# Moving a ScalarE copy from the start of one pass to the end of the pass before, and spreading TensorE's filler matmuls anew, in a gated-delta-net core

## The chip, the cores and the metric

The kernel runs on 1 core of one Trainium2 chip. The metric is the device time in microseconds (us) of one execution, taken as the median of several.

## The reference, cut to what matters

An encoder of two layers works on two sequences of 256 tokens with 1024 features, in float32. Layer 0 mixes tokens with multi-head attention, layer 1 with a gated delta net (GDN) that runs in both directions. Each layer then has a mixture of 16 experts with expert-choice routing, and a gated projection. The change lies inside the GDN of layer 1, whose core is this:

```python
L = jnp.where(strict, jnp.einsum('bhncd,bhnsd->bhncs', kb, k) * decay, 0.0)
T = lax.linalg.triangular_solve(eye + L, eye, left_side=True, lower=True)
u = T @ vb
w = T @ (kb * jnp.exp(gc)[..., None])
...
def step(state, inp):                       # over the chunks of a sequence
    v_new = u_n - w_n @ state
    o_n = qg_n @ state + a_n @ v_new
    state = state * gl_n[..., None, None] + jnp.swapaxes(kg_n, -1, -2) @ v_new
```

The output of the core is gated with `silu(z)`, where `z` is one slice of the input projection `h @ w_in`. This projection of `z` is independent of the core.

## The kernel before

The kernel keeps activations on chip and streams all weights from memory. Each engine has its own instruction list, written out by hand, and semaphores join the lists. An engine works its list strictly in order, so a wait at one instruction holds all that stand behind it.

**The core in passes.** The work of the core is cut into `QS = 4` passes. A pass `q` covers 16 units: 4 heads, two directions, two sequences, of 128 tokens. For every pass the triangular matrix is inverted by doubling. Level 0 is done on VectorE; levels 1 to 4 work inside 32x32 blocks; two more steps (`z5`, `du5`, `dt5` and `z6`, `du6`) join the blocks to 64 and to 128. Then `vn`, `av`, `ks`, `qs` and `st` apply the inverse. The loop `for p in range(QS + 1)` runs levels 0 to 4 of pass `p` and, between them, the joins and the application of pass `p - 1` (`prev`). TensorE, ScalarE and VectorE each have such a loop, in `gdn_pe`, `gdn_act` and `gdn_dve`. A boundary between iterations is called p=0 to p=1, and so on.

**One level.** TensorE transposes the unfinished inverse (`level_turn`, L1414) and multiplies it with the matrix (`level_z`, L1405). ScalarE spreads the transposed inverse into a block-diagonal buffer (`spread_u`, L932, four copies), and VectorE transposes the product (`turn_z`, L2103). TensorE multiplies both (`level_d`, L1427). VectorE puts the result in place and transposes it (`merge`: L2112 and L2087; the latter counts the semaphore `t1_done`), and the next `level_turn` may start.

**Between two passes.** After `level_d(p, 4)` TensorE has `build_qk(p, 2)` and `build_qk(p, 3)` (L1377), `level_turn(p+1, 0)`, `level_z(p+1, 1)`, then `z5(p)` (L1445), which waits for the last `merge` of pass `p`, `level_d(p+1, 1)`, `du5(p)` (L1456), which waits until ScalarE has copied the result of `z5` (`keep`, L964), `dt5(p)` (L1466), the next level, and `z6(p)` (L1480, L1481), which waits for `join64` (L960, L961). On ScalarE `end_levels(q)` (L944) copies the finished 32x32 blocks of pass `q` into the buffer `c_t64`, four copies of 32x256; `join64` adds the off-diagonal blocks to it. `end_levels` waits for `t1_done` of the last level and, from pass 1 on, for `z6` of the pass before, which is the last reader of `c_t64`. `spread_inverse` (L953) copies the same blocks into `c_u`.

**The filler of p=0.** In p=0 there is no earlier pass, and TensorE fills the gaps of the levels with the projection of `z`: eight groups `gate_part(i, k0, k1)` (L1346), of eight matmuls each, from `xt` and a weight slot. Each of these matmuls stands as two records in the trace. ScalarE takes each finished group out with `gate_in(i)` (L885). Groups 5, 6 and 7 are the ones within p=0.

**GpSimd.** The buffer `xt` is used again once the projection is done. The list of GpSimd (POOL) has this at that point:

```python
pool.wait_ge(*s_z.full(8))                       # all eight groups of z are done
pool.memset(flat_xt, 0.0).then_inc(zeroed, 1)    # L699
pool.wait_ge(zeroed, 3)
spread_m(1)                                      # L674, four copies into xt
mask_decay(1)
```

For p=1 and later, `level_z(p, 1)` waits for `spread_m(p)`, and `spread_u(1, 0)` on ScalarE waits for the memset (`zeroed` at 3), since both kinds of block-diagonal buffer lie in `xt` from pass 1 on.

Of the kernel before, what the change touches and what calls it, by code (L numbers as in the profile page):

```python
# [21 lines left out]
KD = D // P  # L22
# [101 lines left out]
def trunk_kernel(nc, x_prompt, x_sample, p_prompt, p_sample, norm_mix_g, norm_ffn_g, norm_ple_g,  # L124
# [4 lines left out]
    with ExitStack() as ctx:  # L129
# [266 lines left out]
        for l in range(2):  # L396
# [3 lines left out]
            prev = lay[0] if l else None  # L400
# [369 lines left out]
        def _(act):  # L770
# [68 lines left out]
            def gdn_act():  # L839
# [41 lines left out]
                def gate_in(i):  # L881

                    f, j = i // 4, i % 4
                    act.wait_ge(*s_z.full(i + 1))
                    act.activation(znat[:, j, 4 * f:4 * f + 4, :], psum[:, apply_banks.bank(s_z, i), :].rearrange("p (h w) -> p h w", h=4),  # L885
                                   ACT.Silu).then_inc(s_z.freed(i)[0], 1)
# [48 lines left out]
                def end_levels(q):  # L935

                    act.wait_ge(t1_done, t1_at(q, LEVELS - 1))
                    if q:
                        act.wait_ge(*core["z6"].full(q))
                    if q == 0:  # L940
                        act.wait_ge(zeroed, 2)
                    for g in range(4):
                        gs, u0 = slice(32 * g, 32 * g + 32), 8 * (g // 2)
                        ins = act.activation(c_t64[gs, :, 32 * (g % 2):32 * (g % 2) + 32], c_t1[q % 2][gs, u0:u0 + 8, :], ACT.Copy)  # L944
                    ins.then_inc(t64_done, 1)
# [52 lines left out]
                for p in range(QS + 1):  # L998
                    live, prev = p < QS, p - 1
                    m_prev = prev % 2  # L1000
                    if live:
                        spread_u(p, 0)
                    if p:
                        end_levels(prev)
                        keep(apply_banks, "z5", prev, c_z5, 32)
                        spread_inverse(prev)
                    else:
                        gate_in(5)
                    if p:
                        join64(prev)  # L1010
                        if p == QS:
                            act.wait_ge(o_sum, 1)
                            act.activation(fac[:, F_Y, :, 0:4], fac[:, F_Y, :, 0:4], ACT.Sqrt).then_inc(o_sqrt, 1)
                    if live:
                        spread_u(p, 1)
                    if p:
                        keep(apply_banks, "z6", prev, c_z6, 64)
                    else:
                        exp_decay(1, 0)
                        exp_decay(1, 1)  # L1020
                    if p >= 2 and p % 2 == 0:
                        for a in range(4):
                            keep(apply_banks, "st", 4 * (p // 2 - 1) + a, c_s[a // 2][:, 4 * (a % 2):4 * (a % 2) + 4, :], P)
                    if p in (1, 2):
                        exp_decay(p + 1, 0)
                    if live:
                        spread_u(p, 2)
                    if p == 0:
                        exp_decay(1, 2)
                        exp_decay(1, 3)  # L1030
                    if p == QS - 1:
                        square_out(0, 0)
                        square_out(0, 1)
                    if p and m_prev == 0:
                        for a in (0, 1):
                            keep(apply_banks, "vn", 4 * prev + a, c_vn[:, 4 * a:4 * a + 4, :], P)
                    if p in (1, 2):
                        exp_decay(p + 1, 1)
                        exp_decay(p + 1, 2)
                    if p and m_prev == 0:  # L1040
                        for a in (2, 3):
                            keep(apply_banks, "vn", 4 * prev + a, c_vn[:, 4 * a:4 * a + 4, :], P)
                    if p == QS - 1:
                        square_out(0, 2)
                        square_out(0, 3)
                    if p and m_prev == 1:
                        for a in range(4):
                            keep(apply_banks, "vn", 4 * prev + a, c_vn[:, 4 * a:4 * a + 4, :], P)
                    if p in (1, 2):
                        exp_decay(p + 1, 3)  # L1050
                    if live:
                        spread_u(p, 3)
                    if p + 1 < QS:
                        start_level(p + 1)
                    if p == 0:
                        gate_in(6)
                        gate_in(7)

                def turned(k):

# [97 lines left out]
        def _(pe):  # L1158
# [143 lines left out]
            def gdn_pe():  # L1302
# [237 lines left out]
                for p in range(QS + 1):  # L1540
                    live, prev = p < QS, p - 1
                    odd = prev % 2
                    build = p in (1, 2)
                    if live:
                        level_turn(p, 0)
                        level_z(p, 1)
                    if p:
                        z5(prev)
                    else:
                        gate_part(5, 0, 5)  # L1550
                    if live:
                        level_d(p, 1)
                    if p:
                        du5(prev)
                        dt5(prev)
                    else:
                        gate_part(5, 5, KD)
                        gate_part(6, 0, 1)
                    if live:
                        level_turn(p, 1)  # L1560
                        level_z(p, 2)
                    if p:
                        z6(prev)
                    else:
                        gate_part(6, 1, 4)
                        build_kk(1, 0)
                    if p >= 2:
                        for a in range(4):
                            if p % 2 == 0:
                                new_state(p - 2, a)  # L1570
                            else:
                                with_state("qs", p - 2, a)
                            if p == QS and a == 1:
                                du6(prev)
                    if live:
                        level_d(p, 2)
                    if 1 <= p < QS:
                        du6(prev)
                    elif p == 0:
                        gate_part(6, 4, 7)  # L1580
                        build_kk(1, 1)
                    if build:
                        build_kk(p + 1, 0)
                    if live:
                        level_turn(p, 2)
                        level_z(p, 3)
                    if p and odd:
                        for a in range(4):
                            with_state("ks", prev, a)
                    elif p:  # L1590
                        for a in (0, 1):
                            new_values(prev, a)
                    else:
                        gate_part(6, 7, KD)
                        gate_part(7, 0, 2)
                        build_kk(1, 2)
                    if build:
                        build_kk(p + 1, 1)
                        build_kk(p + 1, 2)
                    if live:  # L1600
                        level_d(p, 3)
                    if p == QS:
                        for a in range(4):
                            with_state("qs", prev, a)
                    if p:
                        for a in range(4) if odd else (2, 3):
                            new_values(prev, a)
                    else:
                        gate_part(7, 2, 5)
                        build_kk(1, 3)  # L1610
                    if build:
                        build_kk(p + 1, 3)
                    if live:
                        level_turn(p, 3)
                        level_z(p, 4)
                    if p == QS:
                        turn_heads(0)
                    if p:
                        for a in range(4):
                            attend(prev, a)  # L1620
                    else:
                        gate_part(7, 5, KD)
                    if live:
                        build_qk(p, 0)
                        build_qk(p, 1)
                        level_d(p, 4)
                        build_qk(p, 2)
                        build_qk(p, 3)
                def project_heads(i, half):
# [791 lines left out]
```

## Time and profile before

| what | value |
|---|---|
| median of 3 runs | 1781.27 us (1781.05 to 1781.36) |
| profiled execution, its own time | 1781.27 us |
| span of the profiled execution | 1779.5 us |
| TensorE (PE) busy | 1638.2 us, 92% |
| VectorE (DVE), ScalarE (ACT), GpSimd (POOL) busy | 515.8, 461.7, 67.5 us |
| iteration p=0 of the core | from 973.5 to 1016.7 us of the span |
| passes p=1 to p=4 | up to about 1166 us |

PE is the matrix engine, and PEld is the loading of its weights, which overlaps with it. A row of a timeline gives the start in the span, the busy time, engine, line of the kernel, operation and operands, then the number of instructions merged into the row, and in brackets how long the engine stood idle before it and what ended that.

### The profile page before, as it was taken

The page shows a single profiled execution, that of the slowest core. Times are in us where ns is not written, and L with a number is a line of the kernel's source. Part 1 is how long each engine was busy: PE and PEld are TensorE (multiplying, and loading weights), DVE is VectorE, ACT ScalarE, POOL GpSimd, SP SyncE. Part 2 cuts the span into 40 slices and gives each one's busy share as a digit, 9 for nine tenths or more (in the row PEclk, how much of TensorE's full clock was granted, in tenths as well). Part 3 has the DMA queues.
Part 4 walks back from the last instruction along what each step waited for, and adds up shares of the span by engine and source line. Part 5 has one row for each costly group of instructions (what it writes and reads, how often), then busy time and mean ns, then how long its engine had stood idle before and what let it go on. Part 6 is the DMA issues. An engine that isn't in the chain of part 4 may idle for free.

```text
span 1779.5 us, 20467 instructions
## 1 busy us (share of the span) xinstructions
PE 1638.2 (92%) x8671; PEld 774.6 (44%) x8671; DVE 515.8 (29%) x998; ACT 461.7 (26%) x1008; POOL 67.5 (4%) x87
## 2 busy tenths in 40 slices
PE   7999799998899979999999999897999988999887
PEld 4464344342243324444445678753443422433233
DVE  3562401120111213254451356633111202112032
ACT  3232211110011105432225575442111010111053
POOL 2000000000000000000004231000000000000000
PEclk9999899999999999999999999998999999999999
DMA  7007269999999995012120000273699999999931
GB/s 249 1 6 325 119 282 427 428 428 428 427 424 429 427 424 188 0 48 93 49 95 1 1 3 2 96 300 150 245 427 428 427 428 427 424 429 426 427 138 47
DMA packets 50906, 450.30 MB, mean 253 GB/s; under 512 B 4931, under 2 KB 7199, under 8 KB 25599
## 3 DMA queue, kind: packets, MB, share of 16 engines
q1 hardware_dynamic: 50288, 448.67, 60.9%
q8 instruction: 69, 1.13, 0.3%
q0 software_dynamic: 288, 0.22, 0.0%
q14 instruction: 22, 0.18, 0.0%
q10 hardware_dynamic: 239, 0.09, 0.0%
HBM read 446.87 MB, written 2.10 MB: 252 GB/s over the span
## 4 chain that ended last, share of the span: by engine, by line
PE 74%; DMA 16%; ACT 5%; DVE 3%; issue 1%; SPq 1%; DVEq 0%; ACTq 0%
PE banks L1726 26%; PE banks L1184 23%; DMA ring<-in_moe_w_up 7%; DMA ring<-in_moe_w_down 5%; PE banks L1377 4%; DMA ring<-in_moe_w_gate 3%; PE banks L1635 3%; PE banks L1346 3%; PE banks L1752 3%; PE banks L1705 3%; PE banks L1780 2%; PE banks L1267 1%; PE banks L1386 1%; PE banks L1405 1%; PE banks L1427 1%
## 5 line engine op out<-in xcount | busy, mean ns | idle before, releaser
L1726 PE MATMUL banks<-ring,misc 128*64 128x512 f32 x2048 | 460.1, 600 | 38.6 <-DMA ring<-in_moe_w_up 21.7
L1726 PEld LDWEIGHTS banks<-ring,misc 128*64 128x64 f32 x2048 | 147.1, 138 | 324.3 <-issue 280.9
L1726 PE MATMUL banks<-ring,hid_t 128*64 128x512 f32 x976 | 218.1, 596 | 17.8 <-DMA ring<-in_moe_w_down 15.1
L1184 PE MATMUL banks<-ring,xt 128*128 128x512 f32 (+1 forms) x448 | 189.8, 586 | 1.1 <-ACT xt L763 0.6
L2357 DVE TENSOR_TENSOR work<-work,banks 128x512 f32<-128x512 f32 x32 | 33.7, 1053 | 483.6 <-PE banks L1726 483.6
L1184 PE MATMUL banks<-xt,ring 128*128 128x512 f32 x384 | 166.7, 594 | 0.0
L1134 ACT ACTIVATE misc<-banks 32x512 f32<-32x512 f32 x64 | 37.5, 586 | 463.7 <-PE banks L1726 463.3
L1726 PEld LDWEIGHTS banks<-ring,hid_t 128*64 128x64 f32 x976 | 68.5, 137 | 158.1 <-issue 136.6
L1184 PEld LDWEIGHTS banks<-ring,xt 128*128 128x128 f32 x448 | 84.9, 190 | 103.9 <-issue 102.9
L1184 PEld LDWEIGHTS banks<-xt,ring 128*128 128x128 f32 x384 | 72.4, 190 | 91.8 <-issue 89.3
L2372 DVE COPY misc<-banks 32x512 f32<-32x512 f32 x64 | 44.2, 691 | 228.6 <-PE banks L1726 228.2
L1121 ACT ACTIVATE work<-banks 128x512 f32<-128x512 f32 x32 | 19.1, 597 | 221.8 <-PE banks L1726 221.8
L2023 DVE SCALAR_TENSOR_TENSOR misc<-misc,conv_w 128x512 f32<-128x512 f32 x96 | 72.2, 752 | 3.4
L1752 PE MATMUL banks<-misc,xt 128*128 128x512 f32 x128 | 62.2, 620 | 5.4 <-ACT misc L1134 3.1
L1705 PEld LDWEIGHTS banks<-xt,xn 128*128 128x128 f32 x512 | 61.5, 202 | 11.3 <-DVE xt L2318 6.4
L1705 PE MATMUL banks<-xt,xn 128*128 128x128 f32 x512 | 62.9, 287 | 3.3 <-DVEq L2321 3.3
L1346 PE MATMUL banks<-ring,xt 128*128 128x512 f32 x128 | 57.5, 598 | 0.0
L1377 PEld LDWEIGHTS banks<-ring 128*128 128x128 f32 x384 | 48.2, 197 | 14.1 <-issue 9.3
L1377 PE MATMUL banks<-ring 128*128 128x128 f32 x384 | 51.2, 284 | 3.1 <-DVE ring L2078 1.4
L2347 DVE TENSOR_TENSOR h<-h,banks 128x512 f32<-128x512 f32 x64 | 43.6, 687 | 14.1 <-PE banks L1752 14.1
L737 ACT ACTIVATE work<-h 128x512 f32<-128x512 f32 x40 | 24.8, 620 | 76.9 <-DVE h L1977 42.6
L1104 ACT ACTIVATE misc<-banks,ffn_gains 128x256 f32<-128x256 f32 x32 | 13.4, 470 | 109.8 <-PE banks L1705 109.8
(311 smaller groups left out, 1515.2 us busy)
## 6 DMA issues: line engine op xcount, KB each, us to landing
ring<-in_moe_w_gate SPq DMA_DIRECT2D x64, 2048.0 KB, 22.2
ring<-in_moe_w_up SPq DMA_DIRECT2D x64, 2048.0 KB, 24.0
ring<-in_moe_w_down SPq DMA_DIRECT2D x58, 2048.0 KB, 25.5
ring<-in_gdn_w_in SPq DMA_DIRECT2D x8, 2048.0 KB, 8.5
ring<-in_ple_w_gate SPq DMA_DIRECT2D x4, 2048.0 KB, 21.4
ring<-in_moe_w_down SPq DMA_DIRECT2D x6, 1024.0 KB, 23.2
ring<-in_mla_w_out SPq DMA_DIRECT2D x2, 2048.0 KB, 23.6
misc<-in_moe_w_down SPq DMA_DIRECT2D x2, 2048.0 KB, 21.3
```

The source lines that it names most:

```text
L1134: ins = act.activation(ybuf[32 * i:32 * i + 32, s, 0:HALF], psum[32 * s:32 * s + 32, 5, :], ACT.Copy)
L1184: mm = pe.matmul(psum[:, banks.bank(st, i), 0:cols], lhs(k), rhs(k), start=(k == 0), stop=(k == n - 1))
L1346: mm = pe.matmul(psum[:, apply_banks.bank(s_z, i), :], xt[:, k, j * P:(j + 1) * P], slot(6 + f, KD, HALF)[:, k, :], start=(k == 0), stop=( ...
L1377: mm = pe.matmul(o, lhs(g), rhs(g), start=True, stop=True)
L1635: mm = pe.matmul(psum[:, banks.bank(s_go, i), :], got[:, k, j * P:(j + 1) * P], gw_out[f][:, k, :], start=(k == 0), stop=(k == KD - 1))
L1705: mm = pe.matmul(o, xn[:, NT * s + t, c0:c0 + P], oh[:, NT * s + t, q * P:(q + 1) * P], start=(t == 0), stop=(t == NT - 1))
L1726: mm = pe.matmul(psum[64 * f:64 * f + 64, bank, :], tokens(4 * kh + k), w[k][:, k, f * HALF:(f + 1) * HALF], start=(kh == 0 and k == 0), s ...
L1752: pe.matmul(psum[:, 6 + g % 2, :], sc[:, q, j, :], ybuf[:, j // NT, f * HALF:(f + 1) * HALF], start=True, stop=True).then_inc(moe_sem["sca ...
L1780: mm = pe.matmul(psum[:, b, :], ptt(l)[:, k, j * P:(j + 1) * P], w_proj(l)[:, k, f * HALF:(f + 1) * HALF], start=(k == 0), stop=(k == 1))
L2023: ins = dve.scalar_tensor_tensor(out=a, in0=x, scalar=w, in1=a, op0=ALU.mult, op1=ALU.add)
L2347: dve.tensor_tensor(hv, hv, psum[:, 6 + g % 2, :], ALU.add).then_inc(moe_sem["scat_free"], 1)
L2372: ins = dve.tensor_copy(ybuf[32 * i:32 * i + 32, s, HALF:D], psum[64 + 32 * s:96 + 32 * s, 5, :])
```

## The change

Two things are moved; no instruction is added or removed.

On ScalarE, `end_levels` of a pass no longer stands in the next iteration, behind `spread_u(p+1, 0)`, but as the last thing of its own iteration, behind `start_level(p+1)` and, in p=0, behind `gate_in(6)` and `gate_in(7)`.

On TensorE, the 24 filler matmuls of p=0 are cut in another way. Before, the gaps took 5, 4, 3, 3, 3, 3 and 3 of them, all ahead of `level_d(0, 4)`. Now they take 5, 3, 2, 2, 2, 2 and 4, and the last 4 stand behind `level_d(0, 4)`, ahead of `build_qk(0, 2)`.

```diff
 def gdn_act():
     for p in range(QS + 1):
                     if live:
                         spread_u(p, 0)
                     if p:
-                        end_levels(prev)
                         keep(apply_banks, "z5", prev, c_z5, 32)
                         spread_inverse(prev)
...
                     if p == 0:
                         gate_in(6)
                         gate_in(7)
+                    if live:
+                        end_levels(p)
 def gdn_pe():
                         gate_part(5, 5, KD)
-                        gate_part(6, 0, 1)
...
-                        gate_part(6, 1, 4)
+                        gate_part(6, 0, 2)
                         build_kk(1, 0)
...
-                        gate_part(6, 4, 7)
+                        gate_part(6, 2, 4)
                         build_kk(1, 1)
...
-                        gate_part(6, 7, KD)
-                        gate_part(7, 0, 2)
+                        gate_part(6, 4, 6)
                         build_kk(1, 2)
...
-                        gate_part(7, 2, 5)
+                        gate_part(6, 6, KD)
                         build_kk(1, 3)
...
-                        gate_part(7, 5, KD)
+                        gate_part(7, 0, 4)
                     if live:
                         build_qk(p, 0)
                         build_qk(p, 1)
                         level_d(p, 4)
+                        if p == 0:
+                            gate_part(7, 4, KD)
                         build_qk(p, 2)
                         build_qk(p, 3)
```

## Rows read from the trace of the kernel before

**Rows 1.** The page: busy time of the engines, and DMA in 40 slices.

```profile
PE 1638.2 (92%) x8671; PEld 774.6 (44%) x8671; DVE 515.8 (29%) x998; ACT 461.7 (26%) x1008; POOL 67.5 (4%) x87
...
DMA  7007269999999995012120000273699999999931
```

**Rows 2.** Waits from 1008 to 1165 us: waiter, releaser, total, times, longest.

```profile
PE banks L1456 <- ACT misc L964: 4.3, 4, 1.2
...
PE banks L1427 <- ACT xt L932: 2.3, 3, 1.3
...
PE banks L1405 <- POOL xt L674: 0.7, 1, 0.7
```

**Rows 3.** Timeline of PE, in p=0 and at the boundary to p=1.

```profile
980.88 3.70 PE L1346 MATMUL banks<-ring,xt 128*128 128x512 f32 x8
...
1008.96 2.84 PE L1346 MATMUL banks<-ring,xt 128*128 128x512 f32 x6
...
1013.51 1.08 PE L1427 MATMUL banks<-xn,misc 128*32 128x128 f32 x32
...
1018.09 1.08 PE L1405 MATMUL banks<-xt,misc 128*32 128x128 f32 x32 [0.70 <-POOL xt L674]
1019.10 1.11 PE L1445 MATMUL banks<-misc,ring 32*32 32x32 f32 x64
...
1022.21 1.01 PE L1456 MATMUL banks<-misc 32*32 32x32 f32 x58 [0.99 <-ACT misc L964]
...
1028.06 1.08 PE L1427 MATMUL banks<-xt,misc 128*32 128x128 f32 x32 [1.26 <-ACT xt L932]
```

**Rows 4.** Timeline of ACT at the same boundary.

```profile
1017.43 2.39 ACT L932 ACTIVATE xt<-banks 32x512 f32<-32x512 f32 x4 [1.50 <-PE banks L1414]
1019.84 1.69 ACT L944 ACTIVATE misc<-misc 32x256 f32<-32x256 f32 x4
1021.56 0.60 ACT L964 ACTIVATE misc<-banks 128x512 f32<-128x512 f32 x1
1022.18 2.54 ACT L953 ACTIVATE ring<-misc 32x512 f32<-32x512 f32 x4
...
1025.53 2.39 ACT L932 ACTIVATE xt<-banks 32x512 f32<-32x512 f32 x4
```

**Rows 5.** Timeline of POOL at the same boundary.

```profile
1011.86 3.51 POOL L699 MEMSET xt<- 128x4096 f32 x1 [35.61 <-PE banks L1346]
1015.44 2.60 POOL L674 COPY xt<-ring 32x512 f32<-32x512 f32 x4
```

**Rows 6.** Timeline of DVE, ACT and PE at p=1 to p=2.

```profile
1054.92 0.71 DVE L2087 STREAM_TRANSPOSE misc<-misc 128x512 f32<-128x512 f32 x1
...
1055.29 2.39 ACT L932 ACTIVATE xt<-banks 32x512 f32<-32x512 f32 x4 [5.50 <-PE banks L1414]
...
1057.70 1.69 ACT L944 ACTIVATE misc<-misc 32x256 f32<-32x256 f32 x4
1057.82 1.08 PE L1427 MATMUL banks<-xt,misc 128*32 128x128 f32 x32 [0.52 <-ACT xt L932]
...
1060.07 1.01 PE L1456 MATMUL banks<-misc 32*32 32x32 f32 x58 [1.16 <-ACT misc L964]
```

**Rows 7.** Timeline of ACT at p=3 to p=4.

```profile
1134.24 1.69 ACT L944 ACTIVATE misc<-misc 32x256 f32<-32x256 f32 x4 [4.19 <-DVE misc L2087]
```

**Rows 8.** Timeline of PE: a slow `level_z`, and two long gaps elsewhere.

```profile
748.53 1.09 PE L1166 MATMUL banks<-ident,xn 128*128 128x128 f32 x8 [2.48 <-ACT xn L746]
...
1107.13 1.93 PE L1405 MATMUL banks<-xt,misc 128*32 128x128 f32 x32
...
1559.27 3.53 PE L1726 MATMUL banks<-ring,misc 128*64 128x512 f32 x8 [4.81 <-DMA ring<-in_moe_w_up]
```

**Rows 9.** Windows: busy of PE, PEld, DVE, ACT, POOL, then PE's granted clock, DMA.

```profile
1559.50:1562.90 3.40, 3.40 (x10) 0.98 (x8) 0.00 (x0) 0.00 (x0) 0.00 (x0) 0.50 1.01 429
1105.50:1108.90 3.40, 3.40 (x51) 2.62 (x47) 1.68 (x4) 3.31 (x7) 0.00 (x0) 0.50 0.02 5
```

## The prediction

> **What bounds the kernel now.** I read the page first, then the waits of the core, then the timelines of the engines around each place that the diff touches, and last the granted clock. On the page the reader is to see that PE is busy for 1638.2 us of 1779.5, and that DMA is idle while the core runs and at its full share after it [rows 1]. The expert stage behind the core starts from the core's end, since its weights go into buffers that the core frees, so I take it that a microsecond gained or lost on PE's path through the core moves the end by one. The waits of the core show where PE stands still at pass boundaries: 4.3 us in four waits of `du5` for ACT's copy of `z5`, 2.3 us in three waits of `level_d` for `spread_u`, and once 0.7 us of `level_z` for POOL [rows 2]. ACT works in order, so what stands ahead of the awaited copy on its list matters. At p=0 to p=1 that is `end_levels`: `z5` starts at 1019.10 and lasts 1.11, so its result is there at 1020.21, but ACT is in `end_levels` until 1021.53, copies at 1021.56, and `du5` starts only at 1022.21 [rows 3, 4]. That is what the edit on ACT aims at. But the same boundary has a second chain, of POOL: the last group of z ends at 1008.96 + 2.84 = 1011.80, the memset of `xt` starts at 1011.86, the copies into it run from 1015.44 to 1018.04, and `level_z(1, 1)` starts at 1018.09, 0.05 behind them [rows 3, 5]. This chain has no slack at all: whatever delays the last group of z delays `level_z(1, 1)`.
>
> **The change at p=0 to p=1.** Number and size of the matmuls stay. One filler matmul is 3.70 - 2.84 = 0.86 us, a run of four against a run of three [rows 3]. Within p=0, PE has work in every gap, and with one filler less in most gaps the levels simply follow each other sooner; the ACT part of a level is 2.39 us [rows 4] and the gap still holds two fillers and a `build_kk`, so I cost that at nothing. If this cover were too thin, each of the five thinned gaps could add some tenths. `level_d(0, 4)` then comes four fillers earlier, at 1013.51 - 3.44 = 1010.1. Level products take PE 1.01 until the next starts (1018.09 to 1019.10 [rows 3]), so the last four fillers begin at 1011.1 and end 3.70 later, at 1014.8, where the last group of z ended at 1011.80. So z is complete 3.0 us later. Behind this event stand POOL's memset, its copies, `mask_decay(1)`, and on ACT `gate_in(7)`, then the moved `end_levels(0)`, then `spread_u(1, 0)`.
>
> POOL: memset 1014.9 to 1018.4 (3.51), copies to 1021.0 (2.60) [rows 5], `level_z(1, 1)` at 1021.1 in place of 1018.09, 3.0 later. PE has only `build_qk` and `level_turn(1, 0)` to do from 1014.8; before, `level_z` could have started at 1018.09 - 0.70 = 1017.4, 2.9 behind the time at which `level_d(0, 4)` let the next one go (1013.51 + 1.01) [rows 3], so PE is done with them by 1017.5 at the latest and stands idle for nearly 4 us. ACT: `end_levels(0)` ends at about 1017.2 and is hidden in this wait; `spread_u(1, 0)` waits for the memset, 1018.4, and ends at 1020.8 (2.39), ahead of need. Then `z5` starts 1.01 behind `level_z`, at 1022.1, and ends at 1023.2. ACT is free and copies at once, at 1023.2 in place of 1021.56: 1.7 later. So the `end_levels` that is gone from this chain pays back 1.3 of the 3.0 (1021.53 less 1020.21), and no more. From there ACT's list is the path as before: `spread_inverse` and `join64` up to `spread_u(1, 1)` at 1025.53, whose end releases `level_d(1, 2)` at 1028.06 behind 1.26 us of idle time [rows 3, 4]. With 1.7 more, `level_d(1, 2)` starts at 1029.8. This boundary: **+1.7 us**.
>
> **The change at the later boundaries.** At p=1 to p=2 no filler is moved, but the place of `end_levels` is. It waits for the last transposition of `merge(1, 4)`, which DVE ends at 1054.92 + 0.71 = 1055.63; `spread_u(2, 0)`, free to go at 1055.29 before, now stands behind it [rows 6]. New: `end_levels(1)` 1055.65 to 1057.34 (1.69), `spread_u(2, 0)` to 1059.75 (2.39), `level_d(2, 1)` at 1059.9 in place of 1057.82, 2.07 later, with PE idle for 2.6 us ahead of it. `du5` is next on PE, 1.01 behind, at 1060.9; the copy of `z5`, at 1059.8 to 1060.4, is ready by then, so the wait of 1.16 us for it is gone. Against 1060.07 that is **+0.83 us**. So the edit turns a wait of 1.16 into one that is 2.07 longer, since 1.69 us of copies are put ahead of an operation that PE needs 2.5 us sooner than `z5`'s copy. The wait of `du5` occurs four times with at most 1.2 us each [rows 2], and p=2 to p=3 has the same order and distances as p=1 to p=2, so I count it with **+0.83 us** again. At p=3 to p=4 there is no `spread_u(4, 0)`; `end_levels(3)` stands behind `spread_u(3, 3)` in both versions and waits for DVE [rows 7]: **0**. The copies themselves are as many as before. Sum of the waits: 1.7 + 0.83 + 0.83 = 3.4 us.
>
> **The clock.** The half level, 1.2 GHz, has a price that the trace shows: from 1105.50 to 1108.90 the granted clock is 0.50 [rows 9], and a `level_z` there takes 1.93 us against 1.08 at 2.4 GHz [rows 3, 8]. The new idle time of 4 us at the first boundary has a near relative: after 4.81 us without work, PE's clock is at 0.50 from 1559.50 on [rows 8, 9]; after 2.48 us at 746, the next eight transpositions took a normal 1.09 [rows 8]. I expect the half clock in part of `level_z(1, 1)`, `z5`, `level_d(1, 1)`. Bounds: nothing, or two slowed level products, 2 x 0.85 = 1.7; I take one, 0.85. The new 2.6 us at p=1 to p=2 lies near the gap without a fall, but the clock did fall in the trace at p=2 to p=3 with shorter gaps; bounds again 0 and 1.7, I take 0.7. At p=2 to p=3 the fall is there already, so nothing new. The Trainium skill ("TensorE: Matmul & The Clock Gate", section "HAM oscillation — how this bites in real kernels") says that a long enough pause of the matrix engine brings it back to the half clock, so that the work behind a wait starts slow. By that rule the first boundary pays; without it the sum would be 1784.7. The trace agrees at the gap of 4.81 us, and doesn't settle 2.6 us.
>
> **The sum.** 3.4 + 0.85 + 0.7 = 4.95 us. The profiled execution's own time, 1781.27 us, equals the median (1781.27), so the forecast is 1781.27 + 4.95 = **1786.2 us**, +0.28%. What a measurement of this kernel can tell from no change is about 0.2%, that is 3.6 us: the forecast is outside, but not by much.
>
> **The rivals.**
> - *Waits alone, no new half clock*: +3.4, 1784.7 us. For it: the clock stayed at full through the boundaries of p=0 to p=1 and p=1 to p=2 before, in spite of 0.7, 0.99 and 1.26 us of idle time in a row. Against it: 4 us is much longer. Chance 0.2; it lies on the border of 0.2%.
> - *One boundary less*: when everything behind comes later, the half-clock stretch at 1105.50 may fall elsewhere or not happen (its price there was up to 1.3: one level product 0.85 and transpositions), or the 0.83 at p=2 to p=3 is covered by it. Then 3.4 - 1.3 = +2.1, 1783.4 us. Chance 0.12.
> - *Faster, the edit does what it aims at*: `end_levels` is done while ACT would idle anyway, and the waits of `du5` go. Price: 1.3 at the first boundary and 1.16 at two others, 3.6 us, 1777.7 us. It decides at the last `merge`: `end_levels` would have to be finished when `level_turn(p+1, 0)` releases `spread_u`, at 1055.29, so the transposition would have to end at 1053.6 and not at 1055.63; and at the first boundary POOL's copies would have to end by 1018.0, with z complete 3.0 us later. ACT's 5.50 us of idle time ahead of `spread_u(2, 0)` [rows 6] speaks for it at first sight, but it lies before the event that `end_levels` needs. Chance 0.05.
> - *Worse*: both boundaries pay the full 1.7 for the clock, 1781.27 + 3.4 + 3.4 = 1788.1 or more. Chance 0.05.
>
> **How the numbers follow.** The forecast's own case, waits plus some half clock, has 0.58, and its bounds are 1785.2 to 1787.8. The range goes from the third case (1783.4) to nearly the worst (1788.0), which leaves out under 2 in 10. Faster by over 0.2%: 0.04 (the faster rival, nearly whole). Slower by over 0.2%, above 1784.8: the forecast's case, the worst case, and nearly half of the border case, 0.58 + 0.05 + 0.08 = 0.71. Within 0.2%: 0.25.
>
> **What the changed profile would show.** Last filler of z ending at about 1014.8; memset of POOL at about 1014.9 and its copies ending at about 1021.0; `level_z(1, 1)` at 1021.1, behind some 4 us of idle time released by POOL; the wait of `du5` for the copy of `z5` gone at the first three boundaries and kept at the last; `spread_u(2, 0)` behind `end_levels`, and PE idle for 2.6 us ahead of `level_d(2, 1)` for it; a granted clock of 0.50 within about 1018 to 1025. I am wrong if `level_z(1, 1)` starts by 1019.5, if `level_d(2, 1)` is not later against `level_z(2, 1)` than before, or if a thinned gap of p=0 shows idle time on PE.

## The result and the profile after

The changed kernel takes 1790.73 us (median of 5 runs, 1790.04 to 1790.94) against 1781.10 for the kernel before, 9.6 us more: ratio 1.0054, 95% interval 1.0040 to 1.0067. The forecast was 1786.2 with a range up to 1788.0. The direction was right, the size was not. The profiled execution took 1791.96 us, and that of the kernel before 1781.27.

The page of the changed kernel. PE's busy time rose by 6.7 us although it does the same work [rows 1]:

```profile
span 1790.2 us, 20467 instructions
PE 1644.9 (92%) x8671; PEld 781.4 (44%) x8671; DVE 515.9 (29%) x998; ACT 461.8 (26%) x1008; POOL 67.5 (4%) x87
...
PEclk9999899999999999999999999998999999999999
```

Timeline of PE at p=0 to p=1. The lines of the kernel behind the edit have moved by one: L1406 is `level_z`, L1446 `z5`, L1428 `level_d`, L1457 `du5`.

```profile
1011.56 3.70 PE L1347 MATMUL banks<-ring,xt 128*128 128x512 f32 x8
...
1016.88 0.60 PE L1415 MATMUL banks<-ident,misc 128*128 128x128 f32 x4
1021.54 1.93 PE L1406 MATMUL banks<-xt,misc 128*32 128x128 f32 x32 [4.07 <-POOL xt L674]
1023.41 1.74 PE L1446 MATMUL banks<-misc,ring 32*32 32x32 f32 x64
1025.08 1.94 PE L1428 MATMUL banks<-xt,misc 128*32 128x128 f32 x32
1026.94 1.58 PE L1457 MATMUL banks<-misc 32*32 32x32 f32 x58
...
1030.99 1.94 PE L1406 MATMUL banks<-xt,misc 128*32 128x128 f32 x32
...
1034.65 1.08 PE L1428 MATMUL banks<-xt,misc 128*32 128x128 f32 x32
```

POOL and ACT there:

```profile
1015.32 3.51 POOL L699 MEMSET xt<- 128x4096 f32 x1 [38.62 <-PE banks L1347]
1018.89 2.60 POOL L674 COPY xt<-ring 32x512 f32<-32x512 f32 x4
```

```profile
1015.91 1.70 ACT L944 ACTIVATE misc<-misc 32x256 f32<-32x256 f32 x4
1018.92 2.38 ACT L932 ACTIVATE xt<-banks 32x512 f32<-32x512 f32 x4 [1.31 <-POOL xt L699]
1025.19 0.60 ACT L964 ACTIVATE misc<-banks 128x512 f32<-128x512 f32 x1 [3.88 <-PE banks L1446]
1025.82 2.55 ACT L953 ACTIVATE ring<-misc 32x512 f32<-32x512 f32 x4
1030.05 0.37 ACT L960 ACTIVATE misc<-banks 32x256 f32<-32x256 f32 x1 [1.69 <-PE banks L1467]
...
1031.09 2.39 ACT L932 ACTIVATE xt<-banks 32x512 f32<-32x512 f32 x4 [0.28 <-PE banks L1415]
```

The core starts 0.46 us later in this execution than in the one before (its first `level_turn` at 974.30 against 973.84), which has to be taken off every comparison. Then the chain is the forecast one, to a tenth: z complete at 1015.26, 3.0 late after that correction; POOL's memset and copies behind it, as long as before [rows 5]; `level_z(1, 1)` 3.45 - 0.46 = 2.99 late behind 4.07 us of idle time. What follows is not. `level_z` takes 1.93 in place of 1.08, `z5` 1.74 in place of 1.11 [rows 3], and so on up to `z6`. The windows (columns: length, PE busy, PE's granted clock, DMA share and GB/s) show it; the clock stands at 1.2 GHz, half, for 13.6 us:

```profile
1020.80:1034.40 13.60, 12.86 (x288) 0.50 0.01 4
...
1113.10:1119.80 6.70, 6.70 (x119) 0.50 0.01 2
1147.20:1153.90 6.70, 5.85 (x85) 0.50 0.52 160
```

The kernel before has half clock for 3.4 us at the boundary of the second of these rows [rows 9], and at that of the third:

```profile
1139.60:1143.00 3.40, 3.04 (x37) 0.50 0.09 29
```

Both kernels have 3.4 us more of it late in the core, behind a wait of 2.00 us for DVE (from 1156.7 on before, from 1167.5 on in the changed kernel).

At p=1 to p=2, ACT and then PE. `end_levels(1)` waits for DVE, `spread_u` stands behind it, and PE idles for 2.62 us ahead of `level_d(2, 1)`; the next boundary repeats it with 2.61:

```profile
1062.27 1.69 ACT L944 ACTIVATE misc<-misc 32x256 f32<-32x256 f32 x4 [5.88 <-DVE misc L2088]
1063.98 2.39 ACT L932 ACTIVATE xt<-banks 32x512 f32<-32x512 f32 x4
1066.39 0.60 ACT L964 ACTIVATE misc<-banks 128x512 f32<-128x512 f32 x1
```

```profile
1066.51 1.08 PE L1428 MATMUL banks<-xt,misc 128*32 128x128 f32 x32 [2.62 <-ACT xt L932]
1067.52 1.01 PE L1457 MATMUL banks<-misc 32*32 32x32 f32 x58
...
1111.25 1.08 PE L1428 MATMUL banks<-xt,misc 128*32 128x128 f32 x32 [2.61 <-ACT xt L932]
1114.82 1.11 PE L1415 MATMUL banks<-ident,misc 128*128 128x128 f32 x4
1115.86 1.94 PE L1406 MATMUL banks<-xt,misc 128*32 128x128 f32 x32
```

Where the time went, from the starts of the same instructions in both traces, each difference less the one before it (`turn_heads`, L1528 before, is PE's first work on the finished output of the core):

| stretch, up to the start of | measured | forecast, waits + clock |
|---|---|---|
| `level_d(1, 2)` (1034.65 - 1028.06 - 0.46) | +6.13 | 1.7 + 0.85 |
| `level_d(2, 2)` (1075.82 - 1068.43 = 7.39) | +0.80 | 0.83 + 0.7 |
| `level_d(3, 2)` (1123.47 - 1113.83 = 9.64) | +2.25 | 0.83 + 0 |
| first `turn_heads` behind the core (1172.53 - 1162.13 = 10.40) | +0.76 | 0 |

That is 9.94 us over the core.

### The profile page after: what moved, and what is told of

Same layout as the page of the kernel before. It is cut to its first block, busy times and chain, and to the rows that moved or that the text cites. A ratio compares the mean times of both kernels' runs of the same rounds, so it can differ in the third digit from the quotient of the medians.

```text
span 1790.2 us, 20467 instructions
## 1 busy us (share of the span) xinstructions
PE 1644.9 (92%) x8671; PEld 781.4 (44%) x8671; DVE 515.9 (29%) x998; ACT 461.8 (26%) x1008; POOL 67.5 (4%) x87
## 4 chain that ended last, share of the span: by engine, by line
PE 72%; DMA 16%; ACT 4%; DVE 3%; issue 3%; POOL 1%; SPq 1%; DVEq 0%; ACTq 0%; POOLq 0%
PE banks L1727 26%; PE banks L1185 23%; DMA ring<-in_moe_w_up 7%; DMA ring<-in_moe_w_down 5%; PE banks L1378 4%; DMA ring<-in_moe_w_gate 3%; PE banks L1636 3%; PE banks L1706 3%; PE banks L1753 3%; PE banks L1781 2%; PE banks L1347 2%; PE banks L1268 1%; PE banks L1406 1%; PE banks L1428 1%; ACT xn L737 1%
```

## The experiments

All times are medians, with the kernel before run on the same chip (1780.8 to 1781.3 us in these groups; there are three chips, and the ratio is taken within one). Where no interval is given, a difference of two medians is known to about 2 us: the intervals of the ratios are 3 to 5 us wide, and the core alone starts anywhere from 972.1 to 974.6 us in the profiled executions, though no edit lies ahead of it. The starts inside the traces, each counted from the first `level_turn` of its own core, say more, and are given where they settle something. "Mean clock" is PE's granted clock averaged from 970 to 1175 us of the span, the whole core; 0.01 less means 4.1 us more at half clock. `ident` and `tri` are constants, and the unused matmuls write into PSUM banks that the next product overwrites.

| kernel | time, us | ratio to before (95% interval) | mean clock |
|---|---|---|---|
| before | 1781.1 | | 0.98 |
| changed | 1790.7 | 1.0054 (1.0040 to 1.0067) | 0.93 |
| fillers only | 1787.0 | 1.0035 (1.0022 to 1.0049) | 0.94 |
| `end_levels` only | 1788.5 | 1.0041 (1.0028 to 1.0055) | 0.95 |
| changed, PE kept busy in the first gap | 1789.1 | 1.0041 (1.0027 to 1.0054) | 0.93 |
| changed, shorter first wait | 1788.3 | 1.0043 (1.0027 to 1.0058) | 0.94 |
| changed, PE kept busy in all gaps | 1781.4 | 1.0003 (0.9994 to 1.0012) | 1.00 |
| before, PE kept busy | 1777.8 | 0.9983 (0.9974 to 0.9992) | 0.99 |
| `end_levels` only, PE kept busy | 1780.4 | 0.9995 (0.9986 to 1.0004) | 1.00 |
| fillers only, PE kept busy | 1780.3 | 0.9986 (0.9977 to 0.9995) | 0.99 |
| before, copies on VectorE | 1776.7 | 0.9979 (0.9970 to 0.9988) | 0.97 |
| before, copies on POOL | 1774.1 | 0.9965 (0.9951 to 0.9978) | 0.98 |
| the same, PE kept busy | 1775.0 | 0.9965 (0.9951 to 0.9978) | 0.99 |

**Each half alone.** First the changed kernel with `end_levels` back in its old place:

```diff
-                    if live:
-                        end_levels(p)
...
+                        end_levels(prev)
                         keep(apply_banks, "z5", prev, c_z5, 32)
```

> The filler matmuls as in the changed kernel, end_levels at its old place in ScalarE's list. Theory (most of the loss is the half clock that follows PE's wait of 4 us for GpSimd at the first boundary): level_z(1, 1) again starts 3.0 us late, end_levels(0) is done before z5's result is there, so the first boundary loses the same 6.1 us as the changed kernel; the boundaries p=1 to p=2 and p=2 to p=3 lose nothing. Total +6 to +7 us, 1787 to 1788. Rival (the loss is mostly the new place of end_levels, whose copies delay ScalarE at each boundary): at most +2 us, below 1783.5.

Measured: 1787.0, in the expected range, but by luck of the sum. In its trace `level_z(1, 1)` is 3.0 late as expected; the loss is spread differently: 3.8 us up to `level_d(1, 2)` in place of 6.1, 2.9 more at p=1 to p=2, where nothing was changed and the clock now falls, and 1.4 less at p=2 to p=3, where the half clock of the kernel before is absent. The wait ahead of `level_z(1, 1)` is as long as in the changed kernel, and the half clock with it is half as long:

```profile
1021.14 1.93 PE L1405 MATMUL banks<-xt,misc 128*32 128x128 f32 x32 [4.07 <-POOL xt L674]
```

```profile
1019.90:1026.70 6.80, 5.56 (x134) 0.50 0.01 2
```

Then the kernel before with the ACT edit alone:

```diff
-                        end_levels(prev)
                         keep(apply_banks, "z5", prev, c_z5, 32)
...
+                    if live:
+                        end_levels(p)
```

> end_levels at its new place, the fillers as before. Theory: POOL's chain is as before; at p=0 to p=1 end_levels(0) waits for the last merge (1017.8) and puts spread_u(1, 0) 2 us later, and du5 0.9 us later; the same 0.83 at the next two boundaries: +2.5 us of waits, with no gap on PE over 2.7 us, so little new half clock except where it was before (p=2 to p=3, p=3 to p=4, 0 to 2 us more). Total +2.5 to +4.5 us, 1783.6 to 1785.6. Rival (each move costs in proportion, the clock has no part): 0.83 per boundary and nothing else, +2.5 us exactly. Rival 2 (end_levels was the main loss): +6 us or more.

Measured: 1788.5 (1785.6 to 1790.2), a miss: three times the 2.5 us of waits. Its profiled execution was the fastest of its five, 1785.6. The two halves cost 6.2 and 7.7 us by the medians and 5.9 each by the starts in the traces up to `turn_heads`, together 11.8 and more, where both edits cost 9.9. Of this excess 0.86 was to be expected, since the wait that the ACT edit adds at the first boundary is covered by POOL's when both are made. The rest points to something shared, and both traces show the clock falling at boundaries.

**PE kept busy in the first gap.**

```diff
                     level_banks.claim(pe, st, i)
                     b = level_banks.bank(st, i)
+                    if i == 4:                      # level_z(1, 1)
+                        for _ in range(4):
+                            pe.matmul(psum[:, b, :], ident[:, :], tri[:, :, :], start=True, stop=True)
                     if v == 1:
                         pe.wait_ge(m32_done, 4 * q + 4)
```

> The changed kernel, and ahead of level_z(1, 1), where PE waits about 4 us for GpSimd, four extra matmuls of 128x512 into the bank that level_z overwrites; they compute nothing that is used. They take 3.4 us and fit in the wait. Theory (half clock after the wait): PE's clock stays at full through the first boundary, level_d(1, 2) comes 1.7 to 2.2 us late instead of 6.1, and the total falls by 4 to 4.5 us against the changed kernel, to about 1786.5. Rival (the waits themselves are longer than I worked out, or PE's small matmuls are slow for another cause): added work on PE gains nothing, 1790.7 or more.

Measured: 1789.1. The total missed, the first boundary did not. Timeline of PE (here L1404 the unused matmuls, L1409 `level_z`, L1431 `level_d`):

```profile
1016.08 3.60 PE L1404 MATMUL banks<-tri,ident 128*128 128x512 f32 x8
1020.31 1.08 PE L1409 MATMUL banks<-xt,misc 128*32 128x128 f32 x32 [0.64 <-POOL xt L674]
...
1028.99 1.08 PE L1431 MATMUL banks<-xt,misc 128*32 128x128 f32 x32 [0.40 <-ACT xt L932]
...
1060.85 1.93 PE L1431 MATMUL banks<-xt,misc 128*32 128x128 f32 x32 [2.61 <-ACT xt L932]
```

The clock stays at full, and `level_d(1, 2)` starts at 1028.99 where it started at 1028.06 before; this core began 0.77 us earlier, so it is 1.70 late: the forecast 1.7. But the clock then falls at the next boundary, behind the 2.61 us, where it had not fallen in the changed kernel: the stretch to `level_d(2, 2)` loses 4.9 us in place of 0.8, and up to `turn_heads` it is 9.7 us late, where the changed kernel was 9.9. In this execution the filled gap saved next to nothing in sum while the next one was open. It is one of the slower ones (1790.2); two of the five took 1786.6 and 1786.7, the time expected, at a higher mean clock of the whole execution (0.982 and 0.983 against 0.980). They left no trace, so whether the next fall was missing in them isn't shown.

**A shorter wait.** The clearing of `xt` is shared out, and ACT's `spread_u` waits for VectorE's half (`ux_zeroed`):

```diff
-                pool.memset(flat_xt, 0.0).then_inc(zeroed, 1)
+                pool.memset(flat_xt[:, 0:2048], 0.0).then_inc(zeroed, 1)
...
                         merge(p, 4)                 # VectorE
+                        if p == 0:
+                            dve.wait_ge(*s_z.full(8))
+                            dve.memset(flat_xt[:, 2048:4096], 0.0).then_inc(ux_zeroed, 1)
```

> The changed kernel, but POOL clears only the half of xt that its own copies need (1.75 us in place of 3.51), and VectorE, idle then, clears the half that spread_u needs. Theory (the half clock follows the length of PE's wait): the wait ahead of level_z(1, 1) shrinks from 4.1 to 2.3 us, level_z(1, 1) comes 1.2 us late against the kernel before; ScalarE's chain is ahead, so the copy of z5 loses nothing. The clock falls for less than 13.7 us or not at all; total 3 to 7 us below the changed kernel, 1784 to 1788. Rival (the half clock comes at such a boundary with any gap over 2 us, and its length doesn't depend on the gap): only 1.8 us below the changed kernel, 1789.

Measured: 1788.3, 2.5 below the changed kernel; the least that I expected was 3, and the rival said 1.8, so the total doesn't decide between them. The trace says more: with 2.36 us of wait the half clock at the first boundary lasted 3.4 us in place of 13.6, and `level_d(1, 2)` is 1.11 late after the start's shift of 0.72. But 3.7 us went at the next boundary, with the clock down again.

**PE kept busy in all gaps, and the control.** The same four matmuls, and a helper that puts others into the bank of the next product:

```diff
+                def idle_work(name, i, n):
+                    if n:
+                        apply_banks.claim(pe, core[name], i)
+                    for _ in range(n):
+                        pe.matmul(psum[:, apply_banks.bank(core[name], i), :], ident[:, :], tri[:, :, :], start=True, stop=True)
...
                         z5(prev)
+                        idle_work("du5", prev, [0, 0, 2, 2, 0][p])
...
+                        idle_work("du5", prev, [0, 0, 0, 0, 1][p])
                         du5(prev)
...
+                        idle_work("z6", prev, [0, 0, 0, 0, 1][p])
                         z6(prev)
...
+                    if p == 1:
+                        idle_work("du6", prev, 1)
                     if live:
                         level_d(p, 2)
```

> The changed kernel with unused matmuls in every gap over 0.9 us up to p=4: four ahead of level_z(1, 1), one ahead of level_d(1, 2), two ahead of level_d(2, 1) and level_d(3, 1), one ahead of du5(3) and z6(3), each into a bank that the next product overwrites. With one gap filled the half clock moved on to the next boundary and the total stayed. Theory (idle time sets the clock, and the clock is what lies beyond the 3.4 us of waits): full clock through the core up to the gap at the last attend; 3.4 us of waits less about 2 us for the two half-clock stretches of before: 1782 to 1784. Rival (the falls have another trigger, such as the small products of 32 columns, with or without gaps): the clock still falls in the core, 1787 or more.

> Control: the kernel before with one unused matmul ahead of each of the du5 that waits about 1 us, one ahead of level_d(1, 2) and one ahead of z6(3). Theory: the stretches at half clock at 1105.5 and 1139.6 (3.4 us each) go, -1 to -3 us, 1778 to 1780. Rival (extra work only gets in the way, or the clock has another trigger): 1781 or more with the stretches still there.

The control is the kernel before with the same helper; its counts ahead of `du5` are `[0, 1, 1, 1, 1]` and none ahead of `level_d(p, 1)` and `level_z(1, 1)`. Measured: 1781.4 and 1777.8. Windows over the core, first the changed kernel:

```profile
970.00:1175.00 205.00, 188.71 (x2730) 0.93 0.07 22
```

then with all gaps filled:

```profile
970.00:1175.00 205.00, 197.08 (x2793) 1.00 0.10 35
```

and the control:

```profile
970.00:1175.00 205.00, 197.29 (x2801) 0.99 0.11 42
```

The first is a little below the range that I gave (1782 to 1784), the second at the lower end of its own (1778 to 1780). This settles the cause. Work that computes nothing makes the changed kernel 9.3 us faster, and the kernel before 3.5 us (3.0 by the ratio). With the gaps filled, the two kernels differ by 1781.4 - 1777.8 = 3.6 us, against the forecast sum of waits of 3.4. By the intervals that is 3.6 give or take about 2, and the control still has 3.4 us of half clock behind the wait of 2.00 us for DVE, so the traces are the better measure. The first `level_turn`, `level_d(1, 2)` and `level_d(3, 2)`, first with all gaps filled, then in the control:

```profile
972.80 0.60 PE L1418 MATMUL banks<-ident,misc 128*128 128x128 f32 x4
1028.91 1.08 PE L1431 MATMUL banks<-xt,misc 128*32 128x128 f32 x32
...
1114.83 1.08 PE L1431 MATMUL banks<-xt,misc 128*32 128x128 f32 x32
```

```profile
972.43 0.60 PE L1414 MATMUL banks<-ident,misc 128*128 128x128 f32 x4
1026.67 1.08 PE L1427 MATMUL banks<-xt,misc 128*32 128x128 f32 x32 [0.21 <-ACT xt L932]
...
1111.08 1.08 PE L1427 MATMUL banks<-xt,misc 128*32 128x128 f32 x32
```

Up to `level_d(1, 2)` the edits cost 56.11 - 54.24 = 1.87 us, up to `level_d(3, 2)` 142.03 - 138.65 = 3.38, the forecast 3.4. The rest is clock: about 6 us of the 9.6 by the medians, 9.9 - 3.4 = 6.5 by the traces.

**The halves at full clock.**

> end_levels at its new place, fillers as before, and unused matmuls in PE's gaps: two ahead of level_d(1, 1), (2, 1), (3, 1), one ahead of level_d(1, 2), du5(3) and z6(3). With full clock only the waits are left, so this measures them against the kernel before with its gaps filled (1777.8). Theory: 0.86 + 0.83 + 0.83 = 2.5 us: 1780.3. Rival (part of the 7.6 us that this edit alone cost is no matter of the clock): over 1782.5.

> The fillers as in the changed kernel, end_levels at its old place, and unused matmuls in PE's gaps: four ahead of level_z(1, 1), one ahead of level_d(1, 2), du5(1), du5(2), du5(3) and z6(3). Theory: only the 1.7 to 1.9 us at p=0 to p=1 are left, against 1777.8: 1779.5 to 1779.7. With the 2.5 us of the other edit, of which 0.86 lie at the same boundary and are covered, that makes the 3.6 us measured for both. Rival (the thinned gaps of p=0 cost as well): over 1781.

Edits as in the two kernels above, with the helper (for the first also two ahead of `level_d(1, 1)`, for the second one ahead of `du5` in p=2 to p=4). Measured: 1780.4 and 1780.3, so 2.6 and 2.6 us over the control; expected 2.5 and 1.7 to 1.9. By the starts up to `level_d(3, 2)` it is 2.1 and 2.5. The first fits within what this can tell (the first boundary gave 0.6 where I had 0.86). The second is above by 0.7; its executions spread from 1776.6 to 1780.8, by the ratio it would be only 0.5 over the control, and its profile has a pause of 0.55 us inside `du5` that no engine released, all of the loss being up to `level_d(1, 2)`. The 7.7 us of the ACT edit alone were thus 2 to 3 of waits and about 5 of clock.

**The copies on another engine.** If `end_levels` stands in the way on ACT, it can be given to an engine that idles then. First VectorE, behind `turn_z(p, 1)`:

```diff
-                        end_levels(prev)            # ScalarE
...
                         turn_z(p, 1)                # VectorE
+                    if p:
+                        end_levels(prev)            # with dve.tensor_copy
                     if live:
                         merge(p, 1)
```

> The kernel before, fillers as before, but end_levels taken off ScalarE altogether: VectorE makes these four copies, right behind turn_z(p, 1), where it waits for level_d. Theory (end_levels stood in the way on ScalarE's list, and the right cure is another engine, not an earlier place): du5 no longer waits for the copy of z5 at the first three boundaries, 1.0 to 1.3 us each, and level_d(1, 2) comes 1.3 us sooner; -3.3 to -4 us, about 1777.5; if the half-clock stretch at p=2 to p=3 goes as well, another 1 us less. Rival (the wait moves on to join64 or z6, or VectorE's merge is delayed by the copies): within 1 us of before.

Measured: 1776.7, 3.7 us below the kernel before by the ratio (2.1 to 5.3): in total what I forecast, but by another way. Timeline of DVE at the first and at the second boundary (L2095 are the copies):

```profile
1019.85 3.75 DVE L2095 COPY misc<-misc 32x256 f32<-32x256 f32 x4
...
1059.63 1.14 DVE L2095 COPY misc<-misc 32x256 f32<-32x256 f32 x4
```

and POOL at the first:

```profile
1018.09 5.06 POOL L684 TENSOR_TENSOR ring<-tri,ring 128x512 f32<-128x512 f32 x4
```

Four copies take 1.14 us when POOL is idle and 3.75 while it works. At the first boundary this held up `merge(1, 1)` and brought 2.1 us of idle time on PE, and `level_d(1, 2)` comes 2.0 us later than before, with 6.8 us of half clock from 1023.8 on; the next boundary gained 1.0 by the starts, and the third 2.7, since the half clock of the kernel before is absent there. The Trainium skill ("SBUF — State Buffer", section "SBUF: two separate sides") says that GpSimd and those VectorE instructions that use a second pair of ports share this pair as an exclusive lock, held for a whole instruction. The trace agrees: POOL's four instructions take 1.3 us each; the first three copies took 0.89, 1.26 and 1.26 us, each ending 0.1 to 0.2 us behind one of them, and the fourth, with POOL done, took 0.29. It doesn't show which mode the copies ran in.

Then POOL itself:

```diff
                 spread_m(1)
+                end_levels(0)                       # with pool.tensor_copy
                 mask_decay(1)
                 for q in range(2, QS):
                     decay_terms(q)
                     spread_m(q)
                     mask_decay(q)
+                    end_levels(q - 1)
+                end_levels(QS - 1)
```

> The kernel before, but the four copies of end_levels made by POOL: for pass 0 between spread_m(1) and mask_decay(1), for the others behind mask_decay, where POOL is idle. On VectorE these copies took 3.75 us in place of 1.7 at the first boundary while POOL worked, and held up merge(1, 1) by 2.3 us. Theory: POOL is done with them before join64 needs them at all boundaries, VectorE's merge isn't touched, so 1.0 to 1.5 us less at each of three boundaries and 0.4 at the last; about -4 us of waits, 1776 to 1777, below the version on VectorE if the clock stays up. Rival (POOL is too slow or too late and join64 waits for it): level_d(1, 2) not earlier than before, 1779 or more.

In this kernel, too, ACT's list no longer has `end_levels`. Measured: 1774.1, 7.1 us below the kernel before (by the ratio 6.2, interval 3.9 to 8.7), and 2 below the range that I gave. POOL, then ACT (L969 copies `z5`, L949 is `spread_u`):

```profile
1013.82 2.60 POOL L674 COPY xt<-ring 32x512 f32<-32x512 f32 x4
1016.54 1.76 POOL L699 COPY misc<-misc 32x256 f32<-32x256 f32 x4
...
1052.86 1.75 POOL L699 COPY misc<-misc 32x256 f32<-32x256 f32 x4 [2.36 <-issue]
```

```profile
1018.64 0.60 ACT L969 ACTIVATE misc<-banks 128x512 f32<-128x512 f32 x1 [0.44 <-PE banks L1449]
...
1022.62 2.39 ACT L949 ACTIVATE xt<-banks 32x512 f32<-32x512 f32 x4
```

ACT now idles when `z5` ends, and copies at once. `level_d(1, 2)` comes 1.3 us sooner, the next two boundaries 1.3 and about 2.7 (with the half clock of before gone there), and the mean clock is no lower than before. That the third boundary gave 2.7 and not 1.2 is why it is better than forecast. Last, this version with one unused matmul ahead of `z6(3)` and two ahead of the last `qs` product:

> The kernel with end_levels on POOL (1774.1), and three unused matmuls in the two largest gaps left: one ahead of z6(3), two ahead of the last qs product (2.0 us of waiting for VectorE). Theory: the stretch of 6.8 us at half clock at 1131 goes, -1 to -2 us, 1772 to 1773. Rival (falls go on elsewhere, or the gaps left are too short to matter): 1774, no difference.

Measured: 1775.0, no difference. The stretch at half clock shrank from 6.8 to 3.4 us (at 1133.6) and didn't vanish, and no gain shows. What would keep the clock up there stays open.

## Why the prediction was wrong, point by point

- *The waits.* Right. z complete 3.0 late, `level_z(1, 1)` 2.99 late, 4.07 us idle where nearly 4 was said, 1.70 at the first boundary once the clock is held, 2.09 more for `level_d(2, 1)` against `level_z(2, 1)` (8.69 less 6.60 by the starts) where 2.07 was said, the wait of `du5` gone at three boundaries and kept at the fourth. Sum forecast 3.4; measured with the gaps filled 3.4 by the traces and 3.6 by the medians.
- *p=0 itself at nothing.* Right: `level_d(0, 4)` came 3.43 us sooner, as four fillers make, and no thinned gap shows idle time.
- *p=1 to p=2.* +0.80 measured, of 0.83 for waits; the 0.7 that I added for clock did not occur there in this kernel, though it did with 4.1 us in the one whose first gap was filled.
- *The clock.* This is the step that failed, in two places: "Bounds: nothing, or two slowed level products, 2 x 0.85 = 1.7; I take one", and "At p=2 to p=3 the fall is there already, so nothing new". Forecast 1.55 us over all, measured 9.6 - 3.6 = 6.0 by the medians. Both follow from taking a fall as a fixed short stretch with a fixed price, as at 1105.50 [rows 9]. It is neither. At the long gap the half clock lasted 13.6 us, and at the last two boundaries 6.7 us where it had been 3.4. Nor does the gap alone give the length: with the same 4.07 us in the kernel with the fillers only it was 6.8. And at half clock the path changes hands: ACT's list decided before, with PE waiting for it; now ACT waits 1.69 us for PE (`join64` for `dt5`), and `level_d(1, 2)` starts right behind `z6` with no wait. Every product between the two counts then, not only the two that ACT waits for. From `level_z(1, 1)` to `level_d(1, 2)` it took 13.1 us; with the clock held, 8.9.
- *The kernel before as the base.* I took its time as what the waits give. It carries a clock loss of its own, of which the control recovered 3.5 us by the medians and 2.9 by the starts up to `turn_heads`; my rival "one boundary less" had seen that such a stretch may move, but only one.
- *The rivals.* Only "worse" (1788.1 or more, chance 0.05) covers what was measured, and not by its own mechanism: it let p=0 to p=1 and p=1 to p=2 pay 1.7 each for the clock, where the first paid 6.13 - 1.7 = 4.4 and the second nothing.
- *"I count it with +0.83 again" at p=2 to p=3, and 0 at p=3 to p=4.* The waits did this (+0.73 and +0.13 with the gaps filled); the rest of the measured +2.25 and +0.76 goes with the longer half clock in the windows above.

## What to carry to other kernels

An operation moved to "where its engine idles" must be ready there: `end_levels` was put ahead of `spread_u` in ACT's order but waits for a later event, so the idle time ahead of it was of no use; another engine was the place. Where a dependency moves behind filler work, follow all that waits for the filler's last piece: here a memset on POOL, with no slack. And where PE waits in several places in a row, price the clock over the whole row, not at the longest gap: measure it by filling the gaps with unused matmuls, in the kernel before as well. Compare starts inside the traces, counted from a common instruction, when the totals of single executions differ by as much as the effect.

## What the runs showed of the hardware that was not expected

- Unused matmuls on PE shortened a kernel in which PE is busy for 92% of the span: by 9.3 us in the changed kernel and 3.5 us in the one before, without any real work moved.
- The granted clock fell near the end of one gap of 4.07 us and stayed at 1.2 GHz for 13.6 us, in which PE was busy for 12.9 by the record. With the same gap and the same products behind it in another kernel it stayed there for 6.8 us.
- Filling one gap moved the fall to the next one, 40 us later. The gap there, 2.61 us, brought a fall in that kernel and none in the changed one (2.62 us), with the same instructions around it. What decides between the two stays open.
- Copies of 32x256 on VectorE took 0.89, 1.26 and 1.26 us beside a working POOL and 0.28 without.
